# Attention as one stream over 48 token blocks, with q, k and v projected tokens on partitions

## The chip, the cores and the metric

The kernel runs on all 8 cores of one Trainium2 chip, one batch row of 2048 tokens on each, with no exchange between cores. The metric is the device time of the slowest core, in microseconds (us). The profile is of one execution, on the slowest core.

## The reference

One decoder layer; every core computes this for its row x (2048 x 1024). The attention is a mixture of three groups of 8 heads of 64; group g has its own dilation (1, 4, 16), and each query sees itself and the 128 keys before it at that dilation.

```
ada = silu(c) @ w_ada + b_ada;  shift, scale, gate = split(ada, 3)
h = rms_norm(x, norm_g) * (1 + scale) + shift
z = h @ w_in                                   # 1024 -> 8704
for g, (window, dilation) in enumerate(((128, 1), (512, 4), (2048, 16))):
    q = partial_rope(rms_norm(z_q[g], q_norm_g[g]), positions)   # first 16 of 64 dims turn
    k = partial_rope(rms_norm(z_k[g], k_norm_g[g]), positions)
    o[g], lse[g] = dilated_window_attention(q, k, z_v[g], window, dilation)
attn = sum_g softmax_g(lse) * o[g]
y_a = attn * silu(z_gateA)
y_b = chunked gMLP of z (gelu, layer norm, causal 128x128 mixing) * silu(z_gateB)
merged = sigmoid(z_mA) * (y_a @ w_branch_a) + sigmoid(z_mB) * (y_b @ w_branch_b)
out = x + gate * (merged @ w_out)
```

## The kernel before, in words

Each engine runs its own list of operations in the order in which the program writes them; `Prog.op` adds semaphore waits from the keys that an operation reads and writes (one key per PSUM bank, B0 to B7). `P.barrier()` makes every engine wait for everything issued so far, transfers included.

1. Norm and transposes (0 to 124.8 us). x comes in 16 tiles over POOL's queue, w_ada in six loads over SP's queue into three buffers. PE multiplies c by w_ada, then transposes the normed x into hT (channels on partitions, bf16) by matmuls against the identity (L352); DVE and ACT evacuate them with scale and shift.
2. v (to 211 us). For each group and each of its 16 blocks of 128 tokens (`tok_slice`: tokens of one residue class, so a stride of 1, 4 or 16 in hT), eight 512-column matmuls give v with tokens on partitions (L253 is the line of `mm_group`, used by all projections). The first 512 columns of w_in were loaded early. The rotary tables for 2048 tokens (Ctab, Stab) are made on DVE beside this. A barrier ends it.
3. Attention (to 685.65 us) in 12 rounds, one for each pair of heads (hp) and group. `chunk_block` projects q or k of a head pair for 512 tokens with channels on partitions: stageA is the projection (`zT_block`), a scaled copy on ACT (L526) and three products on DVE (square, times cos, times sin); stageB is three 512-column matmuls (sum of squares per head; identity and permutation for the rotary), logarithm and exponential on ACT (L549, L551), and the product on DVE (L553). `att_units` works in units of up to four (key block, query block) pairs: S_stage has two 64-row matmuls per pair (L598), the exponential (L619) and the mask on DVE (L623); PV_stage has P·V (L637) and the denominators (L640) into two fixed banks, BO and BD; post adds them into acc_n and acc_d (L664, L666). The next round's chunk_blocks are strewn between the units of this round. After group 2, `finalize(hp)` makes the gate of branch A: four projections, exponential, L683, logarithm, exponential, L690, L692. The weights come in 128-column chunks over POOL's queue, two ahead.
4. Branch B (to 816 us), merge of the branches (to 983 us), output projection (to the end): not changed.

What sets the order in the attention:

```
units[0][0]()
for u in range(len(units)):
    if u + 1 < len(units):
        units[u + 1][0]()          # scores of the next unit
    k = -(-(u + 1) * len(nxt) // len(units)) - ci
    for _ in range(k):
        emit_chunk(nxt[ci])        # q/k of the next round
        ci += 1
    units[u][1]()                  # P·V of this unit
    if units[u][2] is not None:
        units[u][2]()              # add into acc
```

## Time and profile before

| | us |
|---|---|
| runs, device time of the slowest core | 1046.74, 1049.2, 1069.1; median 1049.2 |
| profiled execution: span of the slowest core, first to last instruction | 1045.9 |
| spans of the other cores in it | 1030.7 to 1043.4 |
| PE, DVE, ACT, POOL busy in the span | 866.5, 528.8, 513.0, 184.3 |

### The profile page before, as it was taken

Reading aid. Unit: us, or ns where it says so; the run is one execution under the profiler, and the core shown is the slowest. Engines: PE = TensorE matmul, PEld = TensorE weight load, DVE = VectorE, ACT = ScalarE, POOL = GpSimd, SP = SyncE. Lnnn points to the kernel's source line nnn. Section 1 sums busy time; section 2 is a strip of 40 time slices with the busy share of each in tenths; the row PEclk is TensorE's granted clock in tenths of the full one; section 3 lists DMA queues with packets and bytes.
Section 4 is the critical chain, followed back from the end, with each engine's and each line's share of the span. In section 5 each row is a group of like instructions: output and inputs, shape, how many; then the busy total and the mean of one; then the engine's idle time right before and its main releaser. Section 6 shows DMA issues by size and latency. Waiting matters only on the chain.

```text
span 1045.9 us, 16087 instructions; the slowest of 8 cores (1030.7 to 1045.9 us)
## 1 busy us (share of the span) xinstructions
PE 866.5 (83%) x5192; PEld 398.4 (38%) x5192; DVE 528.8 (51%) x1031; ACT 513.0 (49%) x849; POOL 184.3 (18%) x178
## 2 busy tenths in 40 slices
PE   1778599989879687969878787659885899999997
PEld 0115345634334343424433333324332344444443
DVE  1011775057668668667667667554566222222333
ACT  4661734368656676558656666327665222222100
POOL 1110100010000000010001000062333233333376
PEclk9986699999989899889989899669898899999999
DMA  8991162051122122032022010089000623222197
GB/s 234 317 293 27 39 73 41 1 65 13 16 21 21 12 21 22 1 31 20 3 21 22 10 12 1 1 81 142 1 1 1 122 21 38 24 21 21 50 311 243
DMA packets 76193, 63.09 MB, mean 60 GB/s; under 512 B 55888, under 2 KB 62160, under 8 KB 75984
## 3 DMA queue, kind: packets, MB, share of 16 engines
q0 software_dynamic: 63968, 30.86, 21.8%
q1 hardware_dynamic: 9840, 22.83, 8.0%
q10 hardware_dynamic: 2304, 8.39, 2.0%
q8 instruction: 43, 0.70, 0.3%
q14 instruction: 38, 0.31, 0.1%
HBM read 76.14 MB, written 8.39 MB: 81 GB/s over the span
## 4 chain that ended last, share of the span: by engine, by line
PE 58%; ACT 12%; DVE 11%; issue 8%; DMA 8%; POOL 1%; SPq 1%; DVEq 0%; ACTq 0%; POOLq 0%
PE bank L253 28%; DMA arena<-w_ada 6%; PE bank L968 5%; PE bank L970 5%; PE bank L598 3%; DVE arena L666 3%; PE bank L974 3%; PE bank L972 3%; PE bank L637 2%; PE bank L875 2%; ACT arena L619 2%; ACT arena L365 2%; ACT arena L526 2%; ACT arena L549 2%; PE bank L877 1%
## 5 line engine op out<-in xcount | busy, mean ns | idle before, releaser
L253 PE MATMUL bank<-arena 128*128 128x512 bf16 (+1 forms) x1760 | 455.6, 415 | 66.2 <-DMA arena<-w_ada 38.6
L253 PEld LDWEIGHTS bank<-arena 128*128 128x128 bf16 (+1 forms) x1760 | 178.7, 105 | 311.0 <-issue 151.2
L235 POOL DMA_DIRECT2D arena<-w_in x44 | 38.9, 892 | 431.0 <-PE bank L253 337.4
L526 ACT ACTIVATE arena<-bank,arena 128x512 bf16<-128x512 f32 x96 | 66.2, 690 | 69.5 <-PE bank L253 66.4
L619 ACT ACTIVATE arena<-bank 128x512 bf16<-128x512 f32 (+1 forms) x160 | 81.3, 566 | 34.5 <-PE bank L598 29.8
L528 DVE TENSOR_TENSOR arena<-arena 128x512 bf16<-128x512 bf16 x96 | 41.0, 427 | 102.2 <-ACT arena L526 101.2
L981 DVE TENSOR_TENSOR arena<-bank,arena 128x512 f32<-128x512 f32 x32 | 22.1, 692 | 130.5 <-ACT arena L977 122.0
L553 DVE TENSOR_TENSOR arena<-bank,arena 128x512 bf16<-128x512 f32 x96 | 66.5, 692 | 30.5 <-ACT arena L551 30.2
L977 ACT ACTIVATE arena<-bank 128x512 f32<-128x512 f32 x32 | 19.1, 597 | 125.8 <-PE bank L974 125.8
L549 ACT ACTIVATE arena<-bank,arena 128x512 f32<-128x512 f32 x96 | 66.1, 689 | 17.4 <-PE bank L547 15.1
L598 PE MATMUL bank<-arena 64*128 64x128 bf16 x600 | 49.2, 291 | 29.4 <-DVE arena L692 10.8
L623 DVE TENSOR_TENSOR arena<-arena 128x512 bf16<-128x512 bf16 (+1 forms) x160 | 61.0, 409 | 19.3 <-ACT arena L619 16.9
L637 PE MATMUL bank<-arena 128*64 128x128 bf16 x600 | 47.9, 236 | 21.3 <-DVE arena L666 17.3
L968 PE MATMUL bank<-arena 128*128 128x512 bf16 x256 | 62.2, 387 | 3.2 <-issue 3.2
L551 ACT ACTIVATE arena<-arena 128x512 f32<-128x512 f32 x96 | 60.5, 630 | 8.8
L985 POOL TENSOR_TENSOR arena<-arena 128x512 bf16<-128x512 f32 x32 | 40.5, 1265 | 118.8 <-DVE arena L983 118.8
L970 PE MATMUL bank<-arena 128*128 128x512 bf16 x256 | 60.7, 380 | 0.0
L637 PEld LDWEIGHTS bank<-arena 128*64 128x64 bf16 x600 | 34.7, 116 | 58.7 <-issue 58.7
L545 PE MATMUL bank<-arena 128*128 128x512 bf16 x96 | 36.3, 378 | 19.2 <-ACT arena L551 12.2
L480 ACT CAST arena<-bank 128x512 bf16<-128x512 f32 x48 | 27.5, 587 | 48.1 <-PE bank L253 48.1
L640 PE MATMUL bank<-arena 128*64 128x128 bf16 x600 | 46.5, 230 | 0.0
L598 PEld LDWEIGHTS bank<-arena 64*128 64x128 bf16 x600 | 26.0, 115 | 44.3 <-issue 37.0
(115 smaller groups left out, 1123.8 us busy)
## 6 DMA issues: line engine op xcount, KB each, us to landing
arena<-w_in POOLq DMA_DIRECT2D x52, 256.0 KB, 5.2
arena<-w_ada SPq DMA_DIRECT2D x6, 2048.0 KB, 27.0
arena<-x POOLq DMA_DIRECT2D x16, 512.0 KB, 8.4
arena<-x SPq DMA_DIRECT2D x16, 512.0 KB, 6.7
out<-arena ACTq DMA_DIRECT2D x16, 512.0 KB, 6.8
arena<-w_in POOLq DMA_DIRECT2D x4, 1024.0 KB, 14.3
arena<-w_out POOLq DMA_DIRECT2D x2, 1024.0 KB, 12.7
arena<-pos SPq DMA_DIRECT2D x1, 1024.0 KB, 8.5
```

Source lines behind the costliest of these rows:

```text
L253: ins = e.matmul(out_ap, l, r, start=(i == 0), stop=(i == n - 1))
L526: P.op("act", lambda e: e.activation(out=T["zg"], in_=banks[bz], func=AF.Copy, scale=gcol), reads=[B(bz), "gqk"], writes=["zg" + sf])
L549: P.op("act", lambda e: e.activation(out=T["ln"], in_=banks[bs], func=AF.Ln, bias=epsc, scale=1.0), reads=[B(bs), "epsc"], writes=["ln" + sf])
L551: P.op("act", lambda e: e.activation(out=T["rs"], in_=T["ln"], func=AF.Exp, scale=-0.5), reads=["ln" + sf], writes=["ln" + sf])
L553: P.op("dve", lambda e: e.tensor_tensor(out=dstT[:, ts_], in0=banks[br], in1=T["rs"], op=ALU.mult), reads=[B(br), "ln" + sf], writes=["qk% ...
L598: ins = e.matmul(pss[e_][:, j, :], kT[rows, tok_slice(g, kb)], qT[rows, tok_slice(g, qb)], start=True, stop=True)
L619: P.op("act", (lambda ps=pss[e_], pt=pt: (lambda e: e.activation(out=pt[:, 0:nj, :], in_=ps[:, 0:nj, :], func=AF.Exp, scale=0.125)))(), re ...
L623: (lambda pt=pt, mk=mk: (lambda e: e.tensor_tensor(out=pt[:, 0:nj, :], in0=pt[:, 0:nj, :], in1=mk[:, 0:nj, :], op=ALU.mult)))(),
L637: e.matmul(po[orow, sl_, :], V[g][:, kb, hcol], pT[par][e_][:, j, :], start=f_, stop=l_)
L640: ins = e.matmul(pd[orow, sl_, :], ones64, pT[par][e_][:, j, :], start=f_, stop=l_)
L968: e.matmul(banks[bga], wma[:, kc, :], hT[:, kc, ts_], start=(kc == 0), stop=(kc == KC - 1))
L970: e.matmul(banks[bgb], wmb[:, kc, :], hT[:, kc, ts_], start=(kc == 0), stop=(kc == KC - 1))
```

## The change

The stages v and attention become one loop over 48 blocks of 128 tokens, group 1 first, then group 2, then group 0. Step s projects q, k and v of one block for all 8 heads, tokens on partitions (24 matmuls of 512 columns, the block's hT as stationary operand). Norm and rotary are done in that layout: the squares on ACT, their sums per head by a reduction on DVE, logarithm and exponential of 16 values, a scaling on DVE out of PSUM, four rotary operations on POOL on the first 16 of each 64 columns. PE transposes q and k (eight 128x128, into one bank as bf16), and ACT copies them out with the norm gains. One iteration later all 8 heads are attended, in two halves of four heads (h = 0, 1): scores, one exponential over two banks, mask, P·V and denominators into one bank per half, and one accumulation into acc. The loop therefore holds step `it` (projection), `it - 1` (transposes) and `it - 2` (attention). The gates (finA, finB) run in 16 of the last iterations, each for 512 tokens of one head pair. Each of q, k and v has one bank.

The weights now come as 512-column slices: two are loaded early, in the first stage, and four more and the four gate chunks after the first barrier; the three of group 0 at iteration 16 and branch B's at 32. Rotary tables are made for 48 blocks of 128 tokens (about 45 small DVE operations, two sines on ACT) behind the first barrier and ahead of a second one. In the first stage w_ada has two buffers in place of three, and 12 copies of masks are gone. The diff, cut to its core (a line of `...` stands for what is left out):

```diff
         rowb = A.alloc([128, 3 * D], F32)
-        wada_s.append(A.alloc([128, KC, 512], F32))
...
-            elif not early_wv0:
-                early_wv0.append(load_big(0 * 1536 + 1024))
+            elif len(early) < 2:
+                load_w(len(early) + 1, 1536 + (len(early) + 1) * 512)
+                early.append(1)
...
-            s = j % 3
+            s = j % 2
...
+        load_w(0, 1536)
+        load_w(3, 3072)
+        for j in range(2):
+            load_w(4 + j, 3072 + 512 * (j + 1))
+        for hp in range(4):
+            load_chunk(OFF_GATE_A + hp * 128)
...
+        X("dve", "tensor_copy", ["cst"], ["mPD"], out=mPD[:, 1, :], in_=mD)
+        P.barrier()
+
+        ZB = (0, 1, 2)
+        TB = 3
+        SB = (4, 5)
+        PB = (6, 7)
+        steps = [(1, r * 4 + n) for n in range(4) for r in range(4)]
+        steps += [(2, r) for r in range(16)]
+        steps += [(0, n) for n in range(16)]
+        prev = [(s - 4 if s >= 4 else None) for s in range(16)] + [None] * 16 + [None] + list(range(32, 47))
+        NS = 48
+        wsl = {1: (0, 1, 2), 2: (3, 4, 5), 0: (0, 1, 2)}
+
+        def proj(s, role):
+            g, blk = steps[s]
+            sl = tok_slice(g, blk)
+            w = wsl[g][role]
+            mm_group(banks[ZB[role]], [(hT[:, kc, sl], wslot[w][:, kc, :]) for kc in range(KC)],
+                     reads=["ws%d" % w], writes=[B(ZB[role])])
...
+        def sumsq(s, role):
+            q_ = s % 2
+            X("act", "activation", [B(ZB[role])], ["qn%d%d" % (q_, role)], out=qn[q_][:, role, :], in_=banks[ZB[role]], func=AF.Square)
+            X("dve", "tensor_reduce", ["qn%d%d" % (q_, role)], ["ssq%d%d" % (q_, role)],
+              out=ssqk[q_][:, 8 * role:8 * role + 8], in_=qn[q_][:, role, :].rearrange("p (h d) -> p h d", h=8),
+              axis=mybir.AxisListType.X, op=ALU.add)
+
+        def rstd(s):
+            q_ = s % 2
+            X("act", "activation", ["ssq%d0" % q_, "ssq%d1" % q_], ["rs%d" % q_], out=rsqk[q_], in_=ssqk[q_], func=AF.Ln,
+              bias=epsc, scale=1.0 / 64.0)
+            X("act", "activation", ["rs%d" % q_], ["rs%d" % q_], out=rsqk[q_], in_=rsqk[q_], func=AF.Exp, scale=-0.5)
...
+        def scaleqk(s, role):
+            q_ = s % 2
+            X("dve", "tensor_tensor", [B(ZB[role]), "rs%d" % q_], ["qn%d%d" % (q_, role)],
+              out=qn[q_][:, role, :].rearrange("p (h d) -> p h d", h=8), in0=banks[ZB[role]].rearrange("p (h d) -> p h d", h=8),
+              in1=rsqk[q_][:, 8 * role:8 * role + 8].unsqueeze(2).to_broadcast([128, 8, 64]), op=ALU.mult)
...
+            X("pool", "tensor_tensor", keys, ["rta%d" % q_], out=ta, in0=z4, in1=tab(T1), op=ALU.mult)
+            X("pool", "tensor_tensor", keys, ["rtb%d" % q_], out=tb_, in0=z4, in1=tab(T2), op=ALU.mult)
...
+            X("pool", "tensor_tensor", ["rta%d" % q_, "rtb%d" % q_], keys, out=z3[:, :, 0:8], in0=a3[:, :, 0:8], in1=b3[:, :, 8:16], op=ALU.add)
+            X("pool", "tensor_tensor", ["rta%d" % q_, "rtb%d" % q_], keys, out=z3[:, :, 8:16], in0=a3[:, :, 8:16], in1=b3[:, :, 0:8], op=ALU.add)
...
+                for j in range(8):
+                    ins = e.transpose(trb[:, j, :], qn[q_][:, j // 4, (j % 4) * 128:(j % 4) * 128 + 128], ident)
+                return ins
+            P.op("pe", fn, reads=["qn%d0" % q_, "qn%d1" % q_], writes=[B(TB)])
+            X("act", "activation", [B(TB)], ["qr%d" % (s % NQ)], out=qr[s % NQ], in_=trb[:, 0:4, :], func=AF.Copy, scale=gcol[:, 2 * g:2 * g + 1])
+            X("act", "activation", [B(TB)], ["kr%d" % (s % NKV)], out=kr[s % NKV], in_=trb[:, 4:8, :], func=AF.Copy,
+              scale=gcol[:, 2 * g + 1:2 * g + 2])
...
+            X("act", "activation", [B(SB[0]), B(SB[1])], ["pT%d" % i],
+              out=pT[i].rearrange("p e a k q -> p e (a k q)")[:, :, 0:w], in_=ps[:, SB[0]:SB[0] + 2, 0:w], func=AF.Exp, scale=0.125)
...
+            X("dve", "tensor_tensor", ["pT%d" % i], ["pT%d" % i], out=v, in0=v, in1=m, op=ALU.mult)
...
+            o = banks[PB[h]].rearrange("p (n a q) -> p n a q", n=2, a=2)
+
+            def fn(e):
+                ins = None
+                for a in range(2):
+                    for ki_, k_ in enumerate(kb):
+                        for e_ in range(2):
+                            c0 = ((2 * h + a) * 2 + e_) * 64
+                            e.matmul(o[64 * e_:64 * e_ + 64, 0, a, :], vr[k_ % NKV][:, c0:c0 + 64], p[:, e_, a, ki_, :],
+                                     start=(ki_ == 0), stop=(ki_ == nk - 1))
+                for ki_ in range(nk):
+                    for e_ in range(2):
+                        ins = e.matmul(o[64 * e_:64 * e_ + 64, 1, :, :], ones64, p[:, e_, :, ki_, :],
+                                       start=(ki_ == 0), stop=(ki_ == nk - 1))
...
+            if g == 1:
+                X("dve", "tensor_copy", [B(PB[h])], ["acc%d" % h], out=dst, in_=o)
+            else:
+                X("dve", "tensor_tensor", [B(PB[h]), "acc%d" % h], ["acc%d" % h], out=dst, in0=o, in1=dst, op=ALU.add)
...
+        def finA(hp, tb):
+            ts_ = slice(tb * 512, (tb + 1) * 512)
+            mm_group(banks[ZB[2]], [(wchunk[hp][:, kc, :], hT[:, kc, ts_]) for kc in range(KC)], reads=["wc%d" % hp], writes=[B(ZB[2])])
+            X("act", "activation", [B(ZB[2])], ["ft1"], out=ft[1], in_=banks[ZB[2]], func=AF.Exp, scale=-1.0)
+            X("dve", "tensor_tensor", [B(ZB[2]), "acc%d" % (hp // 2), "ft1"], ["ft0"], out=ft[0], in0=banks[ZB[2]], in1=acc[:, 0, hp, ts_], op=ALU.mult)
+            X("dve", "scalar_tensor_tensor", ["ft1", "acc%d" % (hp // 2)], ["ft1"], out=ft[1], in0=ft[1], scalar=1.0, in1=acc[:, 1, hp, ts_],
+              op0=ALU.add, op1=ALU.mult)
+
+        def finB(hp, tb):
+            ts_ = slice(tb * 512, (tb + 1) * 512)
+            X("act", "activation", ["ft1"], ["ft1"], out=ft[1], in_=ft[1], func=AF.Ln)
+            X("act", "activation", ["ft1"], ["ft1"], out=ft[1], in_=ft[1], func=AF.Exp, scale=-1.0)
+            X("dve", "tensor_tensor", ["ft0", "ft1"], ["ya%d_%d" % (hp, tb), "ws4", "ws5"], out=y_aT[:, hp, ts_], in0=ft[0], in1=ft[1], op=ALU.mult)
...
+        fin_at = {}
+        for tb in range(4):
+            for hp in range(4):
+                fin_at[32 + 4 * tb + 6 + hp] = (hp, tb)
+        for it in range(NS + 7):
+            a, b_ = it - 1, it - 2
+            A_, T_, S_ = it < NS, 0 <= a < NS, 0 <= b_ < NS
+            if A_:
+                proj(it, 0)
+                sumsq(it, 0)
+            if S_:
+                scores(b_, 0)
+                mask(b_, 0)
+            if A_:
+                proj(it, 1)
+                sumsq(it, 1)
+            if it - 1 in fin_at:
+                finB(*fin_at[it - 1])
+            if S_:
+                scores(b_, 1)
+                mask(b_, 1)
+            if A_:
+                rstd(it)
+                scaleqk(it, 0)
+                scaleqk(it, 1)
+                rope(it)
+                proj(it, 2)
+                vevac(it)
+            if S_:
+                pv(b_, 0)
+            if T_:
+                transp(a)
+            if S_:
+                accum(b_, 0)
+                pv(b_, 1)
+                accum(b_, 1)
+            if it in fin_at:
+                finA(*fin_at[it])
+            if it == 16:
+                for j in range(3):
+                    load_w(j, 512 * j)
+            if it == 32:
+                load_w(3, OFF_Z_B + 512)
...
         P.barrier()
```

## Rows read from the trace of the kernel before

**Rows 1.** Busy time by stage (length, engines busy, clock, DMA share, GB/s).

```profile
124.78:211.00 86.22, 85.96 (x384) 46.20 (x384) 35.04 (x29) 32.00 (x51) 4.39 (x5) 0.97 0.32 46
211.00:665.30 454.30, 372.80 (x2953) 174.19 (x2954) 317.46 (x658) 295.42 (x502) 22.73 (x26) 0.91 0.17 18
665.30:685.65 20.35, 9.38 (x34) 3.65 (x34) 10.30 (x14) 7.09 (x12) 0.00 (x0) 0.67 0.00 0
...
140.00:200.00 60.00, 60.00 (x279) 33.01 (x278) 27.11 (x17) 24.80 (x38) 0.88 (x1) 1.00 0.21 32
850.00:983.00 133.00, 133.00 (x618) 60.29 (x617) 33.52 (x52) 27.94 (x52) 41.56 (x36) 1.00 0.21 21
```

**Rows 2.** The chain of waits in order of time: start us, us, what.

```profile
124.78 85.98 PE bank L253 x384
```

**Rows 3.** Timeline, attention: start us, us, instructions, idle time before.

```profile
278.35 0.25 PE L637 MATMUL bank<-arena 128*64 128x128 bf16 x2 [1.02 <-DVE arena L666]
...
278.92 0.64 PE L598 MATMUL bank<-arena 64*128 64x128 bf16 x8
...
279.49 1.90 PE L253 MATMUL bank<-arena 128*128 128x512 bf16 x8
...
281.23 0.38 PE L545 MATMUL bank<-arena 128*128 128x512 bf16 x1
...
281.49 0.69 ACT L526 ACTIVATE arena<-bank,arena 128x512 bf16<-128x512 f32 x1 [0.69 <-PE bank L253]
...
286.44 0.25 PE L637 MATMUL bank<-arena 128*64 128x128 bf16 x2 [1.01 <-DVE arena L666]
```

**Rows 4.** Timeline of PE, the last of the six loads of w_ada.

```profile
81.11 9.62 PE L253 MATMUL bank<-arena 128*1 128x512 f32 x16 [3.91 <-DMA arena<-w_ada]
```

**Rows 5.** Busy time by stretch, two stretches with loads of w_in.

```profile
160.00:165.00 5.00, 5.00 (x25) 2.62 (x23) 4.69 (x4) 1.76 (x3) 0.00 (x0) 1.00 1.12 176
...
695.00:700.00 5.00, 0.10 (x1) 0.00 (x0) 2.10 (x6) 2.18 (x3) 3.25 (x4) 0.73 1.22 113
```

**Rows 6.** Timeline of PE, one group of transposes by matmul ahead of v.

```profile
109.10 0.61 PE L352 MATMUL bank<-arena 128*128 128x128 bf16 x8 [0.79 <-DVE arena L360]
```

**Rows 7.** Groups by line and shape: busy us, mean ns, idle before, releasers.

```profile
L553 DVE TENSOR_TENSOR arena<-bank,arena 128x512 bf16<-128x512 f32 x96 | 66.5, 692 | 30.5 <-ACT arena L551 30.2 <-issue 0.2
L526 ACT ACTIVATE arena<-bank,arena 128x512 bf16<-128x512 f32 x96 | 66.2, 690 | 69.5 <-PE bank L253 66.4 <-DVE arena L533 2.1 <-DVE arena L531 0.9
...
L619 ACT ACTIVATE arena<-bank 128x512 bf16<-128x512 f32 x120 | 64.5, 593 | 31.5 <-PE bank L598 26.8 <-DVE arena L664 2.0 <-DVE arena L533 1.2
...
L623 DVE TENSOR_TENSOR arena<-arena 128x512 bf16<-128x512 bf16 x120 | 48.3, 426 | 16.0 <-ACT arena L619 13.7
...
L985 POOL TENSOR_TENSOR arena<-arena 128x512 bf16<-128x512 f32 x32 | 40.5, 1265 | 118.8 <-DVE arena L983 118.8
...
L666 DVE TENSOR_TENSOR arena<-bank,arena 128x512 f32<-128x512 f32 x32 | 33.9, 1058 | 0.0
...
L301 ACT ACTIVATE arena<-arena 128x1024 bf16<-128x1024 f32 x16 | 16.8, 1053 | 23.4 <-DMA arena<-x 23.3
...
L825 DVE BATCH_NORM_STATS2 arena<-arena 128x6 f32<-128x512 f32 x16 | 11.1, 691 | 31.8 <-ACT arena L823 31.8
...
L304 ACT ACTIVATE arena<-arena 128x1 f32<-128x1 f32 x16 | 4.7, 294 | 1.4
```

**Rows 8.** Timeline of DVE at the last finalize, two blocks.

```profile
669.72 0.69 DVE L683 SCALAR_TENSOR_TENSOR arena<-arena 128x512 f32<-128x512 f32 x1 [2.23 <-ACT arena L681]
...
673.55 0.69 DVE L683 SCALAR_TENSOR_TENSOR arena<-arena 128x512 f32<-128x512 f32 x1
```

**Rows 9.** One line and who waits for it: ns min/median/max.

```profile
L843 DVE TENSOR_TENSOR arena<-arena x16: 692/1564/1570, 699.7 to 791.8; 128x512 f32<-128x512 f32 x16
```

**Rows 10.** Groups by line and shape, loads of activation tables.

```profile
L304 ACT ACT_TABLE_LOAD x1 | 1.3, 1283 | 0.1
...
L549 ACT ACT_TABLE_LOAD x1 | 1.3, 1283 | 0.5 <-PE bank L547 0.5
```

More of the change, by code:

```diff
@@ L173, in build_nc @@
     A = Arena(nc, 206 * 1024)
-    banks = [nc.alloc_psum_tensor("bank%d" % i, [128, 512], F32).ap() for i in range(8)]
+    ps = nc.alloc_psum_tensor("ps", [128, 8, 512], F32).ap()
+    banks = [ps[:, i, :] for i in range(8)]
     def B(i):
@@ L218, in build_nc @@
     TOP16 = A.cap - 8192 - 16384
-    wbig = [A.at(TOP8, [128, KC, 512], BF16), None]
+    TOPW = A.cap - 4 * 8192
+    wslot = [A.at(TOPW + 8192 * i, [128, KC, 512], BF16) for i in range(4)]
+    y_flat = A.off - 4 * S * 2
+    wslot += [A.at(y_flat + 8192 * i, [128, KC, 512], BF16) for i in range(2)]
     TWO_PI = 2.0 * math.pi
@@ L228, in build_nc @@
     wc_i = [0]
-    wb_i = [0]
     def load_chunk(c0):
@@ L237, in load_chunk, with load_w @@
         return wchunk[s], key
[L239 to L246 removed]
+    def load_w(s, c0):
+        P.op("pool", lambda e: e.dma_start(out=wslot[s], in_=win_v[:, :, c0:c0 + 512]),
+             writes=["ws%d" % s], slot="ws%d" % s)
     def mm_group(out_ap, pairs, reads, writes):
@@ L297, in build_nc @@
             x_load(t)
-        early_wv0 = []
+        early = []
         for t in range(NT):
@@ new lines, in X @@
+        def X(eng, meth, reads, writes, *a, **kw):
+            P.op(eng, lambda e: getattr(e, meth)(*a, **kw), reads=reads, writes=writes)
+        acc = A.alloc([128, 2, 4, S], F32)
+        off_ring = A.off
+        NQ, NKV, NPT = 3, 7, 3
+        qr = [A.alloc([128, 4, 128], BF16) for _ in range(NQ)]
+        kr = [A.alloc([128, 4, 128], BF16) for _ in range(NKV)]
+        vr = [A.alloc([128, 512], BF16) for _ in range(NKV)]
+        qn = [A.alloc([128, 2, 512], BF16) for _ in range(2)]
+        rt = [[A.alloc([128, 2, 8, 16], F32) for _ in range(2)] for _ in range(2)]
@@ new lines, in build_nc @@
+        pT = [A.alloc([128, 2, 2, 2, 128], BF16) for _ in range(NPT)]
+        T1 = A.alloc([128, 6, 16, 16], BF16)
+        T2 = A.alloc([128, 6, 16, 16], BF16)
+        ft = [A.alloc([128, 512], F32) for _ in range(2)]
+        mPD = A.alloc([128, 2, 128], BF16)
+        gcol = A.alloc([128, 6], F32)
+        st16 = A.alloc([128, 64], F32)
+        ssqk = [st16[:, 0:16], st16[:, 16:32]]
+        rsqk = [st16[:, 32:48], st16[:, 48:64]]
+        assert A.off <= TOPW, ("attention buffers overlap weights", A.off, TOPW)
@@ new lines, in build_nc, with bc @@
+        ang, yy, kf, cosT, sinT = sc3(0), sc3(1), sc3(2), sc3(3), sc3(4)
+        ki = sc3(5).bitcast(I32)
+        for nm, dst, srcd in (("posi", posi, pos_d), ("frq", frq, freq_d.partition_broadcast(128)),
+                              ("grp", so[:, 160:256], grope_d.partition_broadcast(128))):
+            P.op("sp", (lambda d_, s_: (lambda e: e.dma_start(out=d_, in_=s_)))(dst, srcd), writes=[nm], slot=nm)
+        def bc(ap2, n):
+            return ap2.unsqueeze(2).to_broadcast([128, 48, n])
@@ new lines, in vevac, with kblocks, scores, fn @@
+        def vevac(s):
+            X("act", "copy", [B(ZB[2])], ["vr%d" % (s % NKV)], out=vr[s % NKV], in_=banks[ZB[2]])
+        pt_of = {}
+        pt_i = [0]
+        def kblocks(s):
+            return ([prev[s]] if prev[s] is not None else []) + [s]
+        def scores(s, h):
+            kb = kblocks(s)
+            nk = len(kb)
+            sv_ = [banks[SB[e_]].rearrange("p (a k q) -> p a k q", a=2, k=2) if nk == 2 else
+                   banks[SB[e_]][:, 0:256].rearrange("p (a k q) -> p a k q", a=2, k=1) for e_ in range(2)]
+            def fn(e):
+                ins = None
+                for a in range(2):
+                    for ki_, k_ in enumerate(kb):
+                        for e_ in range(2):
+                            rows = slice(64 * e_, 64 * e_ + 64)
+                            ins = e.matmul(sv_[e_][:, a, ki_, :], kr[k_ % NKV][rows, 2 * h + a, :], qr[s % NQ][rows, 2 * h + a, :],
+                                           start=True, stop=True)
+                return ins
+            P.op("pe", fn, reads=["kr%d" % (k_ % NKV) for k_ in kb] + ["qr%d" % (s % NQ)], writes=[B(SB[0]), B(SB[1])])
+            i = pt_i[0] % NPT
+            pt_i[0] += 1
+            pt_of[(s, h)] = i
+            w = 256 * nk
+            X("act", "activation", [B(SB[0]), B(SB[1])], ["pT%d" % i],
+              out=pT[i].rearrange("p e a k q -> p e (a k q)")[:, :, 0:w], in_=ps[:, SB[0]:SB[0] + 2, 0:w], func=AF.Exp, scale=0.125)
@@ L736, in build_nc @@
+        P.barrier()
+        wv = wslot[3]
         P.barrier()
@@ L1084, in _consts @@
     frl = (fr64 - fr.astype(np.float64)).astype(np.float32)
-    for h in range(2):
-        for d in range(16):
-            freq[64 * h + d, 0] = fr[d % 8]
-            freq[64 * h + d, 1] = frl[d % 8]
+    freq[0, 0:8] = fr
+    freq[0, 8:16] = frl
     return c, freq
```

458 lines of the change are left out of this document (100 added, 358 removed).

## The prediction

> **What bounds the kernel now.** I read the busy time by stage first [rows 1], then the chain of waits [rows 2], then one period of the attention stage on PE [rows 3]. The rows cut out what the change replaces: from 124.8 us (end of the norm of x and its transposes) to 685.65 us (first matmul of branch B), 560.9 us. Its first 86.2 us are v: 384 matmuls back to back, on the chain for 85.98 us [rows 2], so 85.98/48 = 1.79 us per block of eight matmuls at a granted clock of 1.00 (2.4 GHz). The next 454.3 us are attention: PE is shown busy for 373 us, at a mean clock of 0.91, so the stretch swings between 1.2 and 2.4 GHz. One period shows why: eight 64x128 score matmuls occupy 0.57 us, sixteen P·V matmuls 0.57 us, and PE then waits 1.01 us for the vector engine's accumulation into acc [rows 3], because there is one output and one denominator bank. The last 20.4 us is the last finalize, with PE busy for 9.4 us at 0.67. So v is bound by PE, and attention by PE plus the accumulation and the finalize seams, with a clock that falls in the gaps.
>
> **Part 1, ahead of the stream.** The third w_ada buffer goes and a second early load of w_in comes. PE waited 3.9 us for the last of the six loads and then worked 9.6 us on it [rows 4], so the loads, not the buffers, set this pace. A load issued when PE has left a buffer still queues behind the other one, so two buffers cost about 0 to 2 us; the early load shares the DMA engines with the last w_ada load, 0 to 6 us. I take 2 (0 to 8). The mask copies that vanish were far ahead of their use: nothing.
>
> **Part 2, a bubble.** v used to start at once on early weights. Now four loads of 1 MB (as bf16) and four of 0.25 MB, all on POOL's queue, are issued behind the barrier at 124.8 us, and a second barrier behind the tables waits for all of them, although the first step needs only slot 0. Loads of 512 columns ran at 176 GB/s when alone, loads of 128 columns at 113 GB/s [rows 5]: 4.2/0.176 + 1.05/0.113 = 33 us, with about 3 us of issue and landing 36. By one rate or the other throughout it is 30 to 46. The table work (some 45 vector operations on at most 384 elements, none above the 0.69 us of a 512-element one) needs under 30 us beside it. The old v stage hid both; PE now has nothing.
>
> **Part 3, the stream on PE.** Projections: 144 groups x 1.79 = 258 us. Block pairs: 27 steps have two key blocks and 21 one, which makes 54 score groups of eight and 42 of four matmuls; at 0.57 and 0.34 us (half, plus a fixed 0.05) 45 us, and the same columns of P·V again 45 us [rows 3]. Gates: 16 x 1.79 = 29 us. The transposes are new: eight of 128x128 per step. The nearest row, eight 128x128 matmuls against the identity, is shown as 0.61 us with its tail [rows 6]; less than 0.4 would beat the P·V pace, and 1.0 is what the group takes at half clock: 0.55 x 48 = 26 us (19 to 48). Sum 403 us. What goes is the three 512-column matmuls behind each of 96 projections, which were PE time.
>
> **Part 4, whether PE is kept fed.** One step with two key blocks costs PE 3 x 1.79 + 2 x 0.57 + 2 x 0.57 + 0.55 = 8.2 us, with one block 7.3.
> ACT per step: two squares and the copy of v at 0.59, two exponentials of 1024 elements at 1.05 (0.59 with one block), two scaled copies at 0.69, two 16-element operations at 0.29 [rows 7]: 5.8 or 4.9 us.
> DVE: two reductions, two scalings, two masks, two accumulations. The reduction is not in the trace; 0.69 is the 512-element statistics row, with 0.43 (bf16 product) and 1.06 (strided accumulation) as ends. Scaling 0.69; mask of 1024 elements 0.75 (two rows of 0.43 less one fixed part; 1.4 if it runs at the f32 rate); accumulation 1.06 with strides, 0.69 without [rows 7]. That makes 6.4, 5.7 and 5.6 us for the three groups. So neither engine is the bound.
> POOL, the rotary: four operations on 768 elements. The row is 1.27 us for 512 [rows 7]: 1.9 us by element, 5.1 if each costs a full row; I take 2.5. The result is due only at the transposes of the next iteration, some 6.9 us after the rotary can start.
>
> The tight loop is the single q bank: proj(it+1, 0) may not write it before scaleqk(it, 0) has read it. From the end of proj(it, 1): hand-over 0.26 (from the end of PE's turn at 281.23 to ACT's start at 281.49 [rows 3]), square of k 0.59, exponential of the second scores up to 2.0, logarithm and exponential to 2.7 (the k reduction has ended by then), scaling of q to 3.6. PE meanwhile has scores, proj v, P·V, transposes and P·V again: 4.1 us. The loop fits with about 0.4 us to spare, with one key block with about 0.1. I charge 0.2 us per step, 10 us in all (0 to 20). The finA iterations give PE another 1.79 us there and DVE and ACT have room, so those gates are already in the 403.
>
> Ends: the first two steps have no attention to cover the loop, and PE starts at 1.2 GHz: +5. In the last iterations no projection covers the softmax and six finalizes follow each other through one ft pair: the old seam takes 3.83 us per block [rows 8], here with one more product about 4.5. Some 33 us, of which 16 are in the sum: +17. Stream: 403 + 10 + 5 + 17 = 435 us. The loads at iterations 16 and 32 have at least 100 us to land and cost POOL about 0.9 us each: nothing.
>
> **Sum.** 124.8 + 2 + 36 + 435 + (1045.9 - 685.65) = 958 us of span. The median of the runs is 3.3 us above the profiled span: 961 us, 8% faster. The measurement can tell about 2% from no change.
>
> **Two rules against it.** On the slowest of eight working cores, v and merge ran 60 and 133 us with PE always busy at a granted clock of 1.00, 2.4 GHz [rows 1]. The Trainium skill, TensorE: Matmul & The Clock Gate, section Seeing it yourself, says that a third core with dense matmuls on a die takes that die to 13/16 of the full clock. By that rule the stream would be 403 x 3/13 = 93 us longer, 1054 us by an estimate from that page; the trace of before disagrees with it. What a lower clock would do is rival E. A vector product of two SBUF tiles beside a POOL operation has a median of 1.56 us where one of 512 elements needs 0.69 [rows 7, 9]; that is longer by most of a POOL operation. The Trainium skill, SBUF — State Buffer, section SBUF: two separate sides, says that GpSimd and a VectorE operation with two SBUF inputs exclude each other through a shared port pair. By that rule, with rotary beside every second mask, the loop is 0.8 us later and its 0.4 us of slack gone, about 0.4 us in 27 steps, 11 us; by my timeline rotary starts after the masks, and I leave it out.
>
> **The rivals.**
> B, the q loop instead of PE sets the step. A reduction at 1.06, a mask at 1.4 or a mask that waits for POOL would do it; against it, each alone eats little more than the slack. With 1 us more per step: 961 + 48 = 1009 us.
> C, slower: activation tables. Square, Exp, Ln and Copy alternate on ACT. If Square is not in the table that holds Exp and Ln, each step has four table loads of 1.28 us [rows 10]: ACT 5.8 + 5.1 = 10.9 us per step and the loop two loads longer; the step grows by about 2.6 us: +125, 1086 us. The gain of 88 us is gone from 1.8 us more per step. For it: no row has Square beside Exp. Against it: Square ran beside Sqrt on one load for 16 tiles, and one load served all of Ln, Exp and Copy.
> D, the bubble and the stalls nearly vanish (loads at the fast rate, slack holds, short tail): below 930 us.
> E, the stream does not hold its clock. At the 0.91 of the old attention it costs 403/0.91 - 403 = +40 us, which the range holds; at 0.83, halfway between the 0.67 of the finalize and 1.00, +83 us, 1044 us, no change. For it: transposes and switches between matmul shapes are new in a stream this dense. Against it: the two dense stretches at 1.00 [rows 1], and gaps that are shorter than in the old attention.
>
> **How the numbers follow.** Forecast 0.61 (935 to 985), B 0.20, D 0.06, C 0.06, E 0.07. The predicted time is 961 us. For the range: bubble -6 to +10, transposes -7 to +22, stalls -10 to +10, phase one -2 to +6; not all at once, so 930 below, and up to B with a little more, 1018 above; C, D and E lie outside. Faster by over 2% (below 1028): forecast, D and most of B, 0.86. Within 2%: E and the end of B, 0.07. Slower: C, and a rotary that takes POOL over 9 us per step, 0.07.
>
> **What would show it.** PE idle for some 36 us from 124.8 us, ended by a DMA of w_in. Then steps of 8.2 to 8.5 us (group 1), 7.3 to 7.5 (group 2), then above 8.2, at a clock near 1.00; DVE and ACT 65 to 80% busy; no table loads inside the stream; a stream of about 435 us with a loose tail of 30. I am wrong if proj(it, 0) waits for DVE in most steps (B), if transposes wait for POOL, if ACT shows loads (C), or if the granted clock stays near 0.8 (E).

## The result, and the profile after

The changed kernel takes 967.7 us (median of five runs, 966.56 to 976.74). Against the kernel before, the ratio is 0.9248, with a 95% interval from 0.9212 to 0.9285: 7.5% faster. The forecast was 961 us and a range of 930 to 1018. Executions in which one die ran at a lower granted clock than the other are left out of all ratios, though not out of the medians; the first profile of e1 below was such a one, which is why that kernel stands there twice.

The profiled execution has a span of 965.9 us; all row times below are of its slowest core. By stage, with what the prediction gave:

| stage | forecast, us | after, us |
|---|---|---|
| norm and transposes, to the barrier | 126.8 | 131.4 |
| bubble, PE idle | 36 | 40.7 |
| stream up to its last steps | 402 | 388.6 |
| tail of the stream | 33 | 46.9 |
| rest | 360.3 | 358.4 |

The lines are new, since the code is new: L254 is the projections, L519 the transposes, L547 the scores, L585 P·V, L589 the denominators, and L374 a helper through which nearly all DVE, ACT and POOL work is issued. Busy time by stretch (length, busy time of PE, PEld, DVE, ACT, POOL with instructions, granted clock, DMA share, GB/s), the bubble, the stream, its tail and a piece of the stream:

```profile
131.40:172.07 40.67, 0.00 (x1) 0.15 (x3) 15.00 (x51) 2.33 (x3) 7.00 (x8) 0.50 1.02 131
172.07:560.70 388.63, 371.02 (x2973) 196.78 (x3020) 271.59 (x401) 248.63 (x454) 107.32 (x192) 0.99 0.08 12
560.70:606.00 45.30, 25.48 (x141) 9.81 (x142) 20.48 (x31) 17.81 (x28) 2.20 (x4) 0.68 0.00 1
322.60:410.60 88.00, 85.31 (x615) 51.54 (x625) 63.80 (x97) 54.40 (x109) 26.63 (x49) 1.00 0.11 18
```

The old attention had a clock of 0.91 and PE busy for 373 of 454 us [rows 1]; the stream has 0.99 and 371 of 389, and in the middle 1.00. The bubble is plain: PE has nothing, DVE works for 15 us, and the DMA engines are busy throughout (share 1.02).

One step with two key blocks, and behind it the starts of two steps with one, timeline of PE (start us, us, instructions, idle time before; weight loads left out):

```profile
250.10 1.67 PE L254 MATMUL ps<-arena 128*128 128x512 bf16 x7 [0.17 <-issue]
...
251.71 0.40 PE L547 MATMUL ps<-arena 64*128 64x128 bf16 x8
...
252.03 1.92 PE L254 MATMUL ps<-arena 128*128 128x512 bf16 x8
...
256.63 0.62 PE L519 MATMUL ps<-arena 128*128 128x128 bf16 x8
...
257.18 0.41 PE L585 MATMUL ps<-arena 128*64 128x128 bf16 x8
...
257.99 1.67 PE L254 MATMUL ps<-arena 128*128 128x512 bf16 x7 [0.17 <-issue]
...
342.88 1.67 PE L254 MATMUL ps<-arena 128*128 128x512 bf16 x7 [0.20 <-issue]
...
350.20 1.67 PE L254 MATMUL ps<-arena 128*128 128x512 bf16 x7 [0.21 <-issue]
```

From 250.10 to 257.99 it is 7.89 us, and the only gap of PE in it is the 0.17 us ahead of its first group. That is no wait: the program has eight matmuls in this group, and the trace has seven records of it (over the whole run 1608 for 1664 weight loads, with 8.5 us of such gaps). Core 1 shows PE busy without a gap from 322 to 410 us:

```profile
322.00:410.00 88.00, 88.00 (x631) 50.52 (x626) 63.88 (x97) 54.95 (x109) 26.59 (x48) 1.00 0.01 1
```

Score groups take 0.32 us from start to start (251.71 to 252.03), where the kernel before had 0.57 [rows 3]; the transposes take 0.55 (256.63 to 257.18), as forecast from [rows 6]. Added up from start to start, 3 x 1.85 + 2 x 0.32 + 2 x 0.57 + 0.55 = 7.88 us, the whole step. Steps with one key block take 7.31 to 7.32 us (342.88 to 350.20), and those with a gate 10.14.

From these rows the change can be accounted for. Between the first stage and branch B, PE's work falls from 468 us [rows 1] to about 405 (371 + 25 and the unrecorded 8), and its idle time from 93 us to about 71, of which the bubble is 41 and the tail 21. That is 85 us; the first stage gives 7 back, and the rest is 2 shorter.

The chain of waits in the bubble (start us, us, what):

```profile
131.62 3.50 POOL arena L246 x4
135.12 2.56 POOL arena L241 x3
137.68 33.55 DMA arena<-w_in
171.23 0.84 issue
172.07 3.19 PE ps L254 x7
```

POOL needs 6 us to issue the loads, four of 512 columns and the chunks, and the last of them lands 33.55 us after that. The last operation on the tables, timeline of DVE:

```profile
157.08 0.49 DVE L374 COPY arena<-arena 128x128 bf16<-128x128 bf16 x2
```

The tables were done at 157.6 us, so the loads end the bubble.

The finalizes in the tail, timeline of PE; each group of eight is one gate projection:

```profile
584.63 3.57 PE L254 MATMUL ps<-arena 128*128 128x512 bf16 x8 [1.75 <-DVE arena L374]
589.95 3.57 PE L254 MATMUL ps<-arena 128*128 128x512 bf16 x8 [1.74 <-DVE arena L374]
595.26 1.89 PE L254 MATMUL ps<-arena 128*128 128x512 bf16 x8 [1.74 <-DVE arena L374]
599.78 2.66 PE L254 MATMUL ps<-arena 128*128 128x512 bf16 x8 [2.63 <-DVE arena L374]
607.55 4.44 PE L254 MATMUL ps<-arena 128*128 128x512 bf16 x12 [5.11 <-DVE arena L374]
```

They follow each other by 4.5 to 5.3 us. PE waits for the ft pair on DVE, and at the low clock its eight matmuls take 3.57 us instead of 1.89.

### The profile page after: what moved, and what is told of

The parts are those of the page before. It is cut to its first block, busy times and chain, and to the rows that moved or that the text cites. A ratio compares the mean times of both kernels' runs of the same rounds, so it can differ in the third digit from the quotient of the medians.

```text
span 965.9 us, 15093 instructions; the slowest of 8 cores (946.2 to 965.9 us)
## 1 busy us (share of the span) xinstructions
PE 791.1 (82%) x4908; PEld 381.5 (39%) x4988; DVE 472.3 (49%) x801; ACT 446.7 (46%) x769; POOL 274.7 (28%) x352
## 4 chain that ended last, share of the span: by engine, by line
PE 65%; DMA 12%; ACT 9%; DVE 6%; issue 6%; POOL 2%; SPq 0%; DVEq 0%; ACTq 0%; POOLq 0%
PE ps L254 36%; DMA arena<-w_ada 7%; PE ps L896 6%; PE ps L898 6%; DMA arena<-w_in 5%; ACT arena L374 3%; DVE arena L374 3%; PE ps L902 3%; PE ps L900 3%; PE ps L585 3%; PE ps L547 2%; ACT arena L360 2%; PE ps L519 2%; PE ps L589 1%; PE ps L803 1%
## 5 line engine op out<-in xcount | busy, mean ns | idle before, releaser
L254 PE MATMUL ps<-arena 128*128 128x512 bf16 (+1 forms) x1704 | 440.1, 406 | 118.2 <-DMA arena<-w_in 45.8
L254 PEld LDWEIGHTS ps<-arena 128*128 128x128 bf16 (+1 forms) x1760 | 185.6, 113 | 324.3 <-issue 174.0
L374 ACT ACTIVATE arena<-ps 128x512 bf16<-128x512 f32 (+2 forms) x208 | 137.8, 705 | 145.8 <-PE ps L254 137.0
L374 POOL TENSOR_TENSOR arena<-arena 128x256 f32<-128x256 bf16 x192 | 105.9, 562 | 314.8 <-DVE arena L374 301.1
L374 DVE TENSOR_TENSOR arena<-ps,arena 128x512 bf16<-128x512 f32 (+1 forms) x176 | 124.1, 758 | 39.6 <-ACT arena L374 38.0
L374 DVE TENSOR_REDUCE arena<-arena 128x8 f32<-128x512 bf16 x96 | 65.9, 686 | 88.4 <-ACT arena L374 88.4
L374 DVE TENSOR_TENSOR arena<-arena 128x1024 bf16<-128x1024 bf16 (+4 forms) x137 | 73.9, 547 | 32.0 <-ACT arena L374 28.0
L913 POOL TENSOR_TENSOR arena<-arena 128x512 bf16<-128x512 f32 x32 | 40.5, 1265 | 118.8 <-DVE arena L911 118.8
L374 ACT ACTIVATE arena<-ps,arena 128x512 bf16<-128x512 bf16 x96 | 60.7, 685 | 14.8 <-PE ps L519 14.6
L896 PE MATMUL ps<-arena 128*128 128x512 bf16 x252 | 61.8, 387 | 3.1 <-issue 2.8
L898 PE MATMUL ps<-arena 128*128 128x512 bf16 x249 | 60.4, 381 | 0.5 <-issue 0.2
L374 ACT ACTIVATE arena<-arena 128x16 f32<-128x16 f32 (+2 forms) x130 | 46.1, 355 | 30.2 <-DVE arena L374 24.3
L585 PE MATMUL ps<-arena 128*64 128x128 bf16 x600 | 35.5, 228 | 9.9 <-DVE arena L374 9.9
L896 PEld LDWEIGHTS ps<-arena 128*128 128x128 bf16 x256 | 25.3, 99 | 34.0 <-issue 4.8
L803 PE MATMUL ps<-arena 128*128 128x512 bf16 x120 | 33.4, 421 | 5.5 <-DMA arena<-w_in 4.4
L898 PEld LDWEIGHTS ps<-arena 128*128 128x128 bf16 x256 | 25.2, 99 | 31.0 <-issue 1.4
```

The costliest lines, as they stand in the source:

```text
L254: ins = e.matmul(out_ap, l, r, start=(i == 0), stop=(i == n - 1))
L374: P.op(eng, lambda e: getattr(e, meth)(*a, **kw), reads=reads, writes=writes)
L585: e.matmul(o[64 * e_:64 * e_ + 64, 0, a, :], vr[k_ % NKV][:, c0:c0 + 64], p[:, e_, a, ki_, :], start=(ki_ == 0), stop=(ki_ == nk - 1))
L803: e.matmul(banks[bu], wug[:, c, kc, :], hT[:, kc, ts_], start=(kc == 0), stop=(kc == KC - 1))
L896: e.matmul(banks[bga], wma[:, kc, :], hT[:, kc, ts_], start=(kc == 0), stop=(kc == KC - 1))
L898: e.matmul(banks[bgb], wmb[:, kc, :], hT[:, kc, ts_], start=(kc == 0), stop=(kc == KC - 1))
```

## The experiments

Theory: PE sets the step (the stream is as long as PE's work), the bubble is w_in's loads, and the losses against the forecast lie at the ends. Rivals: the q loop or POOL sets the step, the tables set the bubble, and the time that was gained against the forecast inside the stream comes from something other than PE's work.

**e0.** The changed kernel unaltered, on the chip of e2, e4 and e6; the others ran on two more.

> The changed kernel once more, unaltered, so that the small differences of its neighbours are read on one chip. Every theory: 966 to 970 us, span 963 to 967 us, first stage to about 131 us, stream from about 172 us to about 607 us.

Measured: 968.09 us, ratio 0.9261 (0.9236 to 0.9285). The kernel before took 1046 to 1047 us (medians) beside the experiments on each of the three chips, so that all can be read against 967.7 us within a few us.

**e3, the dropped matmuls back.**

```diff
+                for j in range(6):
+                    e.matmul(banks[TB], ident, hT[:, j, 0:512], start=True, stop=True)
                 for j in range(8):
                     ins = e.transpose(...)
```

> Each of the 48 steps gets six more matmuls of 512 columns on TensorE, ahead of the step's transposes and into their bank, where the transposes overwrite them: 288 in all, as many as the stage that was dropped had; the output is unchanged. Theory: TensorE sets the length of a step, so that each of these costs its own time: 48 x 6 x 0.216 us = 62 us, about 1030 us, slightly slower or equal to the kernel before. Rival: the steps are set by VectorE, ScalarE or GpSimd, and the matmuls vanish in TensorE's waits: less than 20 us, under 988 us.

Measured: 1018.92 us, ratio 0.9745 (0.9724 to 0.9766), so +51. Timeline of PE, one step with one key block:

```profile
338.75 1.47 PE L519 MATMUL ps<-arena 128*128 128x512 bf16 x6
...
340.06 0.61 PE L521 MATMUL ps<-arena 128*128 128x128 bf16 x8
...
340.94 1.95 PE L254 MATMUL ps<-arena 128*128 128x512 bf16 x8
...
347.36 1.47 PE L519 MATMUL ps<-arena 128*128 128x512 bf16 x6
```

A step is 8.61 us here (338.75 to 347.36), 1.29 more than before the edit; that is the six matmuls, 6 x 0.216 = 1.30. Steps with two key blocks grow as much, from 7.88 to 9.18. The steps with a gate grow only from 10.14 to 10.86, since there PE had a wait of 0.51 us for DVE that the matmuls fill, which takes some 5 us off the 62; and behind the last transposes the tail is 37.0 us instead of 41.5, which was not tested further. That is most of the difference between 62 and 51. PE sets the steps, and the 288 matmuls that went with the old stageB were worth about this; no run takes back the other 30 us of the gain.

**e4, a DVE operation more in the q loop.**

```diff
+            if role == 1:
+                X("dve", "tensor_reduce", ...)   # the k reduction a second time
```

> The reduction of k's squares on the vector engine is done twice (0.69 us more in the loop that frees q's bank, same result). Theory: PE sets the step and the loop has about 0.8 us to spare in steps with two key blocks and 0.25 us in those with one; so only the 21 steps with one key block grow, by about 0.5 us each: +10 us, 977 us. Rival: the loop sets every step, +0.75 us x 48 = +36 us, 1003 us.

Measured: 984.39 us, ratio 0.9413 (0.939 to 0.9437), +16. Timeline of PE, steps with one key block:

```profile
336.42 1.92 PE L254 MATMUL ps<-arena 128*128 128x512 bf16 x8 [0.76 <-DVE arena L374]
...
344.36 1.92 PE L254 MATMUL ps<-arena 128*128 128x512 bf16 x8 [0.59 <-DVE arena L374]
```

These steps are 7.94 us, 0.63 longer, and PE now waits for DVE; most of those with two key blocks are 7.99, 0.1 longer, and those with a gate are not longer. Over the stream that adds up to 16 us, where 10 were expected. The added reduction is 0.69 us, so the loop had about 0.1 us of slack with one key block (0.69 less 0.63) and 0.6 with two, less than the 0.25 and 0.8 of the expectation. Rival B was that near: with one slow operation more on DVE, the loop takes over the steps with one key block.

**e5, more rotary on POOL.** Three of the four products are done twice.

```diff
+            X("pool", "tensor_tensor", keys, ["rta%d" % q_], ..., op=ALU.mult)
+            X("pool", "tensor_tensor", keys, ["rtb%d" % q_], ..., op=ALU.mult)
+            X("pool", "tensor_tensor", keys, ["rta%d" % q_], ..., op=ALU.mult)
```

> GpSimd does three of its four rotary products twice in each step (2.5 to about 4.8 us a step). Theory: the rotary has some 6.8 us of cover behind the step's attention and GpSimd is busy for about a third of a step, so that it costs nothing or, where the masks now come later, a few us: 966 to 976 us. Rival: GpSimd or the two-step pipeline around it sets the pace, and its 2.3 us appear in each of the 48 steps: +110 us, about 1075 us.

Measured: 970.2 us, ratio 0.9278 (0.9264 to 0.9293). POOL's turn grows from 2.5 to between 4.4 and 4.9 us, and the steps stay at 7.89 and 7.32 us: the cover is real. Groups by shape (busy us, mean ns, idle before), the 512-element mask on DVE in e5 and then in the changed kernel:

```profile
L374 DVE TENSOR_TENSOR arena<-arena 128x512 bf16<-128x512 bf16 x42 | 21.5, 511 | 0.0
...
L374 DVE TENSOR_TENSOR arena<-arena 128x512 bf16<-128x512 bf16 x42 | 17.4, 415 | 0.0
```

The mean of 511 ns mixes two kinds. The second mask of each step meets no POOL operation and takes 412 to 417 ns, as in the changed kernel, where none of the 42 meets one. The first mask now begins beside one, and 20 of these 21 take 554 to 712 ns. One of them, timeline of POOL and DVE in e5:

```profile
337.75 0.67 POOL L374 TENSOR_TENSOR arena<-arena 128x256 f32<-128x256 bf16 x1
...
338.10 0.61 DVE L374 TENSOR_TENSOR arena<-arena 128x512 bf16<-128x512 bf16 x1
```

The POOL operation ends at 338.42 us and the mask at 338.71. In all 20 the mask ends 0.28 to 0.29 us after the POOL operation that was running when it began, however far that one had got. So the mask waits for the end of the running POOL operation; the step has the time for it.

**e8, scores with a stride.**

```diff
-        qr = [A.alloc([128, 4, 128], BF16) for _ in range(NQ)]
+        qr = [A.alloc([128, 128, 4], BF16).rearrange("p t j -> p j t") for _ in range(NQ)]
         # kr likewise
```

> The rotated and transposed q and k tiles are kept with the four head pairs interleaved, so that a score matmul reads its 128 columns and its weights with a stride of four elements, as the kernel before did in its second dilation group; everything else is unchanged. Theory: the 0.57 us that the prediction took for eight score matmuls is the price of that stride (290 ns against 216 ns for a contiguous one), so eight cost 0.57 again, four about 0.3, and the stream grows by 54 x 0.24 + 42 x 0.12 = 18 us: 983 to 990 us. Rival: the short time came from the place of the scores between two projections and not from the layout; then scores stay at 0.33 and the time at 966 to 972 us, or ScalarE's copies, now written with a stride, lengthen the step and show as waits of TensorE for ScalarE.

Measured: 1004.99 us, ratio 0.9614 (0.959 to 0.9637), +37: both the theory and the second half of the rival, together. Groups by shape in e8, the scores and ACT's copies of q and k:

```profile
L547 PE MATMUL ps<-arena 64*128 64x128 bf16 x600 | 51.4, 289 | 22.8 <-ACT arena L374 22.8
...
L374 ACT ACTIVATE arena<-ps,arena 128x512 bf16<-128x512 bf16 x96 | 124.7, 1434 | 15.0 <-PE ps L519 15.0
```

and the same two in the changed kernel:

```profile
L374 ACT ACTIVATE arena<-ps,arena 128x512 bf16<-128x512 bf16 x96 | 60.7, 685 | 14.8 <-PE ps L519 14.6
...
L547 PE MATMUL ps<-arena 64*128 64x128 bf16 x600 | 33.7, 220 | 2.8 <-ACT arena L374 2.8
```

A score matmul is shown as 289 ns instead of 220 (they overlap, so that eight take 0.57 us instead of 0.32), and PE's busy time on them grows by 17.7 us, which is the 18 expected; the copies, written with the stride, go from 685 to 1434 ns and make PE wait for ACT ahead of its scores for 22.8 us instead of 2.8. 17.7 + 20.0 = 37.7 us, about the measured loss. The time fell outside the range of 983 to 990, since the theory had left out the copies. The kernel before shows the same price by group. One line and who waits for it (ns min/median/max), the scores at dilation 1, 4 and 16, each in a stretch with a clock of 1.00:

```profile
L598 PE MATMUL bank<-arena x16: 216/216/226, 245.2 to 248.7; 64*128 64x128 bf16 x16
...
L598 PE MATMUL bank<-arena x8: 279/292/297, 278.9 to 279.3; 64*128 64x128 bf16 x8
...
L598 PE MATMUL bank<-arena x16: 408/418/449, 312.0 to 319.8; 64*128 64x128 bf16 x16
```

Its score operands are slices of qT and kT with that dilation as stride; the stream packs each block once, in the copy behind the transposes. The 0.57 us of [rows 3] was a dilation-4 group.

**e2, three w_ada buffers.**

```diff
+        wada_s.append(A.alloc([128, KC, 512], F32))
-            s = j % 2
+            s = j % 3
```

> w_ada gets its third buffer back (it fits behind rowb), all else as changed. Theory: of the 6.6 us by which the first stage grew, two buffers cost at least 2 us, since PE waits 8.7 us for the third load and 8.0 us for the fifth, and the second early load the rest; the last load of w_ada then lands 2 to 4 us earlier than 87.5 us, and the time falls by as much, to 962 to 964 us. Rival 1, buffers alone: the last load at about 81 us as before, the time 960 us. Rival 2, the early load alone: no change, 966 us.

Measured: 958.5 us, ratio 0.9167 (0.9149 to 0.9185), -9: the 960 of rival 1, not the 962 to 964 of the theory. Timeline of PE, the third, the fifth and the last of the six groups with w_ada, in the changed kernel:

```profile
48.12 8.54 PE L254 MATMUL ps<-arena 128*1 128x512 f32 x16 [8.69 <-DMA arena<-w_ada]
...
74.01 9.24 PE L254 MATMUL ps<-arena 128*1 128x512 f32 x16 [8.00 <-DMA arena<-w_ada]
...
87.55 9.30 PE L254 MATMUL ps<-arena 128*1 128x512 f32 x16 [4.29 <-DMA arena<-w_ada]
```

and in e2:

```profile
44.08 9.61 PE L254 MATMUL ps<-arena 128*1 128x512 f32 x16 [5.52 <-DMA arena<-w_ada]
...
65.66 8.72 PE L254 MATMUL ps<-arena 128*1 128x512 f32 x16 [3.18 <-DMA arena<-w_ada]
...
78.70 9.37 PE L254 MATMUL ps<-arena 128*1 128x512 f32 x16 [4.32 <-DMA arena<-w_ada]
```

The last group starts 8.85 us earlier, and even 2.4 us earlier than in the kernel before [rows 4], with the second early load of w_in still in place. So the third buffer is worth all 9 us, and with it the early load costs nothing. The DMA view shows how (busy tenths in 40 slices of the stretch from 40 to 65 us), first the changed kernel, then e2:

```profile
DMA  9989999989999999899999999963101799959997
```

```profile
DMA  9899999999999899899999999999999999899999
```

With two buffers the engines run nearly dry for about 3 us near 58 us: the next load of w_ada waits for PE to leave its buffer. That is a third of the 9 us. The last load of w_ada is also issued later, at 66.09 us, behind the two early loads of w_in (63.78 and 64.66), and shares the engines with them; in e2 it is issued at 53.77, ahead of them. How much the early loads cost with two buffers was not tested.

**e1, the loads behind the second barrier.** Only slot 0 is loaded ahead of it. What the expectation calls slots of w_ada are slots 3 to 5, which hold columns of w_in.

```diff
         load_w(0, 1536)
-        load_w(3, 3072); load_w(4 + j, ...); load_chunk(...)   # 3 slots, 4 chunks
         ...
         P.barrier()
+        load_w(3, 3072); load_w(4 + j, ...); load_chunk(...)
```

> The loads of the last three w_ada slots and of the gate chunks are issued behind the second barrier instead of ahead of it, so that w_in does not queue behind them when the first stage ends. Theory: the bubble of 40.7 us (131.4 to 172.07) waits for w_in, and the rotary tables are done at 157.6; with w_in earlier the stream starts when the tables are done, about 158, and the kernel takes about 14 us less: 952 to 956 us. Rival 1: what is moved is not what w_in waits for, the stream starts at 170 or later, no change: 966 to 969 us. Rival 2: the stream starts early but the loads, now beside the stream, come late to the second half of w_ada's columns or slow the stream, which gives 5 us or more back: 958 to 966 us.

Measured: 952.03 us, ratio 0.9092 (0.9065 to 0.9119). The stream starts at 151.9 us on its slowest core. The same kernel once more:

> The kernel of e1 once more, for an undisturbed profile. Theory: on the slowest core the stream starts within a few us of 152, with TensorE released by the rotary tables and not by a load of w_in, the stream takes 435 us as in the changed kernel, and the kernel takes 948 to 955 us. Rival 2 of e1: the stream takes 440 us or more, because the loads now run beside it.

Measured: 954.32 us, ratio 0.9129 (0.9087 to 0.9171). Timeline of PE, the start of the stream and the end of its last wait in that run:

```profile
158.93 7.42 PE L254 MATMUL ps<-arena 128*128 128x512 bf16 x24 [33.51 <-DVE arena L374]
...
594.01 6.21 PE L254 MATMUL ps<-arena 128*128 128x512 bf16 x22 [4.99 <-DVE arena L374]
```

Now DVE, with the tables, ends the bubble, at 158.9 us, and the stream is 435.1 us, as long as in the changed kernel (607.55 - 172.07 = 435.5). The loads that were moved cost the stream nothing. Both rivals fall: the last 13 to 14 us of the bubble were the wait of the barrier for loads that the first step doesn't need. What is left of it is the tables', some 28 us, and 7.3 us of that is a wait for the small load of the frequencies (chain of waits in the same run):

```profile
130.62 7.32 DMA arena<-freq
```

**e6, two ft pairs.**

```diff
-        ft = [A.alloc([128, 512], F32) for _ in range(2)]
+        ft = [A.alloc([128, 512], F32) for _ in range(4)]
+            p_ = 2 * (hp % 2)          # ft0, ft1 become ft[p_], ft[p_ + 1]
```

> finA and finB get a second pair of ft tiles, used in turn by head pair. Theory: the last finalizes wait for one another through the one pair (4.5 to 5.3 us each behind the last attention); with two pairs the next gate's exponential and products run beside this one's logarithm, about 2 us less for each of the last four: -6 to -8 us, 959 us. Rival: each finalize's own chain over ACT and DVE and the one bank set the pace, -0 to -2 us, 965 us.

Measured: 960.59 us, ratio 0.919 (0.9167 to 0.9214), -7. Timeline of PE in the tail:

```profile
585.27 1.89 PE L254 MATMUL ps<-arena 128*128 128x512 bf16 x8 [1.75 <-DVE arena L374]
588.91 1.89 PE L254 MATMUL ps<-arena 128*128 128x512 bf16 x8 [1.75 <-DVE arena L374]
592.55 1.89 PE L254 MATMUL ps<-arena 128*128 128x512 bf16 x8 [1.75 <-DVE arena L374]
```

The finalizes are 3.64 us apart instead of 4.5 to 5.3. What is left is the projection and one product on DVE, in turn, through the one bank of the gate. Part of the gain is the clock: it is 0.99 here from 580 to 600 us, where the changed kernel had 0.65 from 584.63 to 607.55 and projections of up to 3.57 us.

**e7, together.** Three w_ada buffers; two ft pairs; the tables computed on DVE and ACT in the first stage, two small operations behind each of its tiles; the loads of slots 0 to 2 issued when the last w_ada load has been used, ahead of the first barrier; no second barrier.

```diff
+            for _ in range(2):
+                if tab_ops:
+                    tab_ops.pop(0)()
...
+        for j in range(3):
+            ... dma_start(out=wslot[j_], in_=win_v[...]), reads=["rowb3"]
...
-        P.barrier()
```

> What the single runs pointed to, together: three w_ada buffers (alone -9 us), two pairs of final accumulators (alone -7 us), the rotary tables computed on VectorE during the first stage, and no second barrier, so that w_in is loaded while the first stage runs and its end starts the stream. Theory: the bubble of 40.7 us nearly vanishes (2 to 5 us stay), and the three add up: 968 - 9 - 7 - 38 = about 914 us, 905 to 920. Rival: w_in's load now competes with w_ada's for the same DMA time, the first stage becomes longer by what the bubble loses, and only part is left: 935 to 955 us.

Measured: 915.96 us (915.33 to 919.93), ratio 0.8771 (0.8747 to 0.8795): 52 us less than the changed kernel, against 54 expected. Timeline of PE (the helper is L281 here):

```profile
123.89 7.78 PE L254 MATMUL ps<-arena 128*128 128x512 bf16 x23 [5.84 <-issue]
...
554.87 9.26 PE L254 MATMUL ps<-arena 128*128 128x512 bf16 x31 [5.00 <-DVE arena L281]
```

The bubble is 5.84 us, from PE's last transpose to the first projection, and most of that is ACT evacuating transposes ahead of the barrier. The rival, loads that compete with w_ada's, could not arise: POOL issued them at 87.68 us, when w_ada was done. The stream is 431.0 us.

## Why the prediction was right

The forecast of the mechanism held: PE sets the step, and the bubble is w_in's loads. That the time came so near is in part luck, since several terms were mis-sized and cancelled: the first stage and the bubble are 9 us longer than forecast, the tail 14 longer, the stream ahead of it 13 shorter. The 3.3 us between span and median, taken over from the kernel before, is 1.8 here.

*The step is PE's.* Right: 7.88 and 7.31 us measured, where PE's sum was 8.2 and 7.3, and e3 shows each added matmul at its own price. Rival B (1009 us) did not come true, but e4 shows how close it was. The slack forecast, 0.4 and 0.1 us, measured about 0.6 and 0.1. The charge of 0.2 us per step, 10 us in all, was not due in most steps, where PE has no wait; the steps with a gate have one for DVE, 0.51 us in each of nine, where the prediction counted on room.

*Scores, 45 us.* Mis-sized: at 0.32 us from start to start (0.21 with one key block) they are 54 x 0.32 + 42 x 0.21 = 26 us. The row taken was a dilation-4 group, whose operands are strided; e8 and the kernel's own rows by dilation show that the layout made it slow. The change packs q and k, and this gain is one that the prediction didn't list. P·V (0.57 us) and the transposes (0.55) were as forecast; a projection takes 1.85 where 1.79 was counted, some 9 us over 144 of them, which takes half of the scores' gain back.

*Phase 1, +2 (0 to 8).* It is +6.6. The step that failed is "the loads, not the buffers, set this pace", with two buffers at 0 to 2 us: e2 gets 9 us from the third buffer. The rows showed PE waiting 3.9 us for a load [rows 4], but with three buffers (e2) each later load was issued 11 us or more before the one ahead of it landed; with two it is 0.8 to 8.5 us, so that the DMA engines run dry once, and the last load comes behind the early ones. That the early load shares the engines with the last load of w_ada, as the prediction said, is seen; what it costs is open.

*The bubble, 36 (30 to 46).* 40.7. The transfers were mis-sized: data moves for about 38 us, from 133 to 171, where 33 was worked out from [rows 5]. While POOL issues the eight loads, 0.9 us each, it is 83 GB/s (131.62 to 137.68), then 156 to 159 us, where 176 was taken, and 123 in the end, where 113 was taken. The 33.55 us of the chain count from the last issue, and their likeness to the 33 is chance. e1 shows that the tables come next, for a start at 152 to 159 us.

*The tail, 33.* It is 46.9. A finalize was taken as 4.5 us; most are 5.3 apart, with a clock of 0.68 in the stretch and projections of up to 3.57 us, and from the last one to branch B it is 7.8. The last blocks' attention has nothing beside it either: the first 24 us of the tail hold only two finalizes. What lets the clock fall there is open, for in e6 it is 0.99 with PE no busier (8.1 of 20 us). e6 returns 7 us.

*The rule on POOL and DVE, 11 us, left out.* Rightly: no mask of the changed kernel meets a POOL operation. The exclusion itself is real, as the masks of e5 show.

*Rival C, activation tables.* Did not come true: Square, Exp, Ln and the copies run on one table. In the profile there is one load at 144 us for the sines and one at 179.72, and none in the rest of the stream.

*Rival E, the clock.* Did not come true: 0.99 in 388.6 us, 1.00 in the 88 us shown above, on the slowest core of eight. The Trainium skill, TensorE: Matmul & The Clock Gate, section Seeing it yourself, would have had 13/16 here; this trace, like that of before, disagrees. The level does exist, beside the two that the opening names: the first profile of e1 has 0.81 on core 0 from 796 to 811 us.

## What to carry to other kernels

A loop in which PE has all the other engines' work one or two iterations behind it is priced by PE's own sum, but write down the slack of the tightest loop through a single bank: here 0.1 us separated "PE-bound" from "bank-bound". The time that such a loop returns is then lost at its ends: what waits for a barrier that also waits for loads not needed yet (14 us), a buffer given up in an earlier stage (9 us) and a chain of small operations through one scratch pair (7 us, part of it the clock), so cost the seams with the same care as the steps. When a price is taken from a row, look whether its operands are laid out as the new ones will be.

## What the runs showed of the hardware

- A matmul of 128 bf16 columns against 64 rows is shown as 216 ns with contiguous operands at a clock of 1.00, 290 with a stride of 4 elements and 418 with 16; eight of them, which overlap, take 0.33, 0.57 and 1.08 us from start to start. Both operands had the stride; which of them costs the time was not tested. The Trainium skill, SBUF — State Buffer, section Door 1: The DMA port swizzle, says that a stride of up to 8 bf16 elements is free because it stays in one 16-byte line. At a stride of 4, 8 bytes, TensorE's operands disagree with it here; that a stride of 16, past such a line, is dearer still agrees with it.
- ACT's copy of 512 elements out of PSUM into a tile with a stride of 4 takes 1434 ns instead of 685.
- Rotary products of 256 and 128 elements a partition cost POOL 669 and 454 ns, where a full one of 512 had 1265 [rows 7], so the four of a step take 2.5 us with their gaps, as was taken.
- A product of two SBUF tiles on DVE that begins beside a POOL operation waits for its end: in e5 the 512-element mask ends 0.28 to 0.29 us after it, and takes 554 to 712 ns instead of 415.
